# Block 1 with a plain output projection and a later store, block 3 with a tile of products moved ahead

## The reference, cut to what matters

```python
def retention_layer(h, w_in, w_out):
    q, k, v, g = jnp.split(h @ w_in, [1024, 2048, 4096], axis=-1)   # 4 heads: q, k 256 wide, v, g 512
    ...                                    # rope, chunkwise recurrence over 64-token chunks, giving o
    o = (o - mean(o)) * rsqrt(var(o) + EPS)                          # per head
    return (o * silu(g)) @ w_out                                     # 2048 -> 1024

h = h + retention_layer(rmsnorm(h, ret_norm), ret_w_in, ret_w_out)
kb, vb = shared_kv(h, kv_norm, w_kv)
h = h + swa_sink_layer(rmsnorm(h, swa_norm), swa_w_in, sinks, swa_w_out, kb, vb)
out = rmsnorm(h, final_norm)
```

## Time and profile before

| | us |
|---|---|
| median of 3 runs (2570.06 to 2570.86) | 2570.57 |
| profiled execution, time | 2570.57 |
| profiled execution, span | 2568.7 |
| PE busy | 2412.4 (94%) |
| PEld busy | 1978.0 (77%) |
| DVE busy | 1476.4 (57%) |
| ACT busy | 680.2 (26%) |
| POOL busy | 429.9 (17%) |

### The profile page before, as it was taken

How to read it: one execution, slowest core, us unless ns; L and a number is a source line. 1 busy time by engine, 2 the same in 40 slices (tenths; PEclk the granted TensorE clock), 3 DMA queues, 4 the chain that set the end, 5 groups by cost and what they waited for, 6 DMA issues and landing times.

```text
span 2568.7 us, 28654 instructions
## 1 busy us (share of the span) xinstructions
PE 2412.4 (94%) x11216; PEld 1978.0 (77%) x11216; DVE 1476.4 (57%) x2034; ACT 680.2 (26%) x1470; POOL 429.9 (17%) x326
## 2 busy tenths in 40 slices
PE   7999999999886869697999999999999999999998
PEld 6888888877675657486888888888888887887886
DVE  6555556586454536365376746557385756556374
ACT  2221312244120202022253312213153312222243
POOL 2112112220452524352001100001001000000000
PEclk9999999999998989898999999999999999999999
DMA  8657575637786858586427887786436987787433
GB/s 350 266 199 307 216 278 212 246 115 302 284 316 245 337 215 335 228 323 239 170 101 256 314 281 263 260 267 239 164 126 224 325 277 257 250 276 253 173 109 147
DMA packets 131833, 625.84 MB, mean 244 GB/s; under 512 B 8864, under 2 KB 9632, under 8 KB 109728
## 3 DMA queue, kind: packets, MB, share of 16 engines
q1 hardware_dynamic: 122864, 588.53, 63.2%
q10 hardware_dynamic: 8880, 36.18, 3.8%
HBM read 471.58 MB, written 153.09 MB: 243 GB/s over the span
## 4 chain that ended last, share of the span: by engine, by line
PE 81%; DVE 7%; DMA 6%; POOL 2%; issue 2%; SPq 1%; ACT 1%; DVEq 0%; ACTq 0%; POOLq 0%
PE ps L686 26%; PE ps L688 25%; PE ps L687 25%; DMA whl<-split_w 2%; DMA whl<-comb_w 2%; PE ps L1195 2%; DVE ff L1955 1%; DMA comb_w<-ff 1%; POOL raw L631 1%; DVE ff L2248 1%; POOL ff L640 1%; PE ps L1205 1%; SPq L468 1%; DVE fr L1658 1%; DVE fr L1654 1%
## 5 line engine op out<-in xcount | busy, mean ns | idle before, releaser
L686 PE MATMUL ps<-whl,xhi 128*128 128x512 f32 (+1 forms) x1088 | 419.0, 385 | 20.5 <-DMA whl<-split_w 18.6
L688 PE MATMUL ps<-whl,xlo 128*128 128x512 f32 (+1 forms) x1088 | 413.3, 380 | 0.0
L687 PE MATMUL ps<-whl,xhi 128*128 128x512 f32 (+1 forms) x1088 | 412.0, 379 | 0.0
L686 PE MATMUL ps<-xhi,whl 128*128 128x512 f32 x768 | 308.4, 402 | 81.4 <-DMA whl<-split_w 63.7
L688 PE MATMUL ps<-xhi,whl 128*128 128x512 f32 x768 | 303.8, 396 | 0.0
L687 PE MATMUL ps<-xlo,whl 128*128 128x512 f32 x768 | 303.4, 395 | 0.0
L686 PE MATMUL ps<-whl,fr 128*128 128x512 f32 x640 | 258.8, 404 | 21.7 <-DMA whl<-comb_w 19.4
L688 PE MATMUL ps<-whl,fr 128*128 128x512 f32 x640 | 255.6, 399 | 0.0
L687 PE MATMUL ps<-whl,fr 128*128 128x512 f32 x640 | 254.2, 397 | 0.0
L686 PEld LDWEIGHTS ps<-whl,xhi 128*128 128x128 f32 x1088 | 206.6, 190 | 58.6 <-DMA whl<-split_w 19.0
L688 PEld LDWEIGHTS ps<-whl,xlo 128*128 128x128 f32 x1088 | 206.3, 190 | 39.0
(11 more groups left out here) (215 smaller groups left out, 3826.8 us busy)
## 6 DMA issues: line engine op xcount, KB each, us to landing
whl<-split_w SPq DMA_DIRECT2D x60, 2048.0 KB, 7.9
whl<-split_w SPq DMA_DIRECT2D x118, 1024.0 KB, 6.8
split_w<-whl SPq DMA_DIRECT2D x44, 2048.0 KB, 7.3
whl<-vg_w SPq DMA_DIRECT2D x64, 1024.0 KB, 6.8
raw<-in_stream SPq DMA_DIRECT2D x44, 1024.0 KB, 9.4
vg_w<-ff SPq DMA_DIRECT2D x32, 1024.0 KB, 7.6
whl<-comb_w SPq DMA_DIRECT2D x32, 1024.0 KB, 6.6
raw<-in_stream SPq DMA_DIRECT2D x50, 512.0 KB, 9.2
```

The source lines that it names most:

```text
L686: pe.matmul(dst, lhs[0], rhs[0], start=start, stop=False)
L687: pe.matmul(dst, lhs[0], rhs[1], start=False, stop=False)
L688: return pe.matmul(dst, lhs[1], rhs[0], start=False, stop=stop)
```

## The change

1. **Block 1, projection.** The seven products go; `one_head` now does for block 1 what it did for block 0 alone: chunks 6 and 7 whole, 96 matmuls, four splits of `y` and eight adds. Gate tiles and transposes go in order 0, 1, 2, 3 and no longer 2, 3, 0, 1. `y_sums_lo` on GpSimd runs only in later blocks.
2. **Block 1, order on SP.** Chunks 6 and 7 are loaded next to each other behind piece 5, then store 4 and piece 0 of the next head. Store 5 of a head is handed on (`last_store`) and issued in the next head behind its chunk 1, with piece 1 behind it, ahead of chunk 2; for the last head, behind the second chunk of the post part. The wait for all stores moves behind the post part's loads.
3. **Block 3.** The first of the two tiles of `vg_product(S1, 15, 1, 0)` is issued ahead of `inner(3)`, the second stays behind `cross(3)`.

```diff
@@ combining_head (SP)
                 for c in range(3):
                     load_split(at, c, split_rows(h, c), CHUNK)
+                    if c == 1 and h > 0:
+                        last_store()
+                        load_piece(h, 1)
...
-                sp.wait_ge(o_mm.sem, at(o_mm, 4))
-                load_comb(t4hl, T4)
-                load_comb(t3hl, T3)
-                for c, q, first in ((6, T1, 0), (7, T2, HALF)):
-                    sp.wait_ge(w_used.sem, at(w_used, c - 1))
-                    load_comb(whl[c % 2][:, :, 0:HALF], q)
-                    sp.dma_start(whl[c % 2][:, :, HALF:].bitcast(F32),
-                                 split_rows(h, 6)[:, :, first:first + HALF]).then_inc(w_ready[c % 2].sem, 16)
-                    if c == 6:
-                        store_piece(4)
-                        if h < HEADS - 1:
-                            load_piece(h + 1, 0)
-                sp.wait_ge(yt_mm.sem, at(yt_mm, 4))
-                sp.dma_start(b22hl.bitcast(F32), split_rows(h, 7)[:, :, HALF:]).then_inc(b22_loaded.sem, 16)
-                store_piece(5)
+                for c in (6, 7):
+                    load_split(at, c, split_rows(h, c), CHUNK)
+                store_piece(4)
                 if h < HEADS - 1:
-                    load_piece(h + 1, 1)
+                    load_piece(h + 1, 0)
+                return lambda: store_piece(5)
@@ post_loads (SP)
+                    if c == 1 and last_store is not None:
+                        last_store()
@@ GpSimd, block 1
-                    y_sums_lo(at)
-                    if b < FAST:
                         comb_piece(at, 5)
+                    else:
+                        y_sums_lo(at)
@@ one_head (PE): winograd() is gone, and for blocks 0 and 1
+                    w_wait(at, 5)
+                    for t in range(TT):
+                        over_tokens(t, t, 5, DV, xs, 4, 4, False, True).then_inc(g_mm.sem if t < 3 else w_used.sem, 1)
+                        if t >= 1:
+                            transpose_y(t - 1)
+                    for n in range(2):
+                        w_wait(at, 7 + n - 1)
+                        w = chunk_view(6 + n, 4)
                         for t in range(TT):
+                            pe.wait_ge(yt_lo.sem, at(yt_lo, t + 1))
+                            for e in range(4):
+                                mm = three(ps[:, 4 * n + t, :], [v[:, e, t * P:(t + 1) * P] for v in ythl],
+                                           [v[:, e, :] for v in w], e == 0, e == 3)
+                            mm.then_inc(out_mm.sem if t < 3 else w_used.sem, 1)
+                            if n == 0 and t == 0:
+                                transpose_y(3)
@@ fast_head (PE), last block only
                     else:
+                        vg_product(S1, 15, 1, 0, (0,), ends=False)
                         pe.wait_ge(v_lo.sem, at(v_lo, 4))
                     inner(3, True)
                     cross(3, False)
-                    vg_product(S1, 15, 1, 0)
+                    vg_product(S1, 15, 1, 0, (1,) if last else (0, 1))
@@ post part (PE)
-                pe.wait_ge(h_add.sem, at(h_add, -8 if first else -2))
+                pe.wait_ge(h_add.sem, at(h_add, -8 if b < FAST else -2))
```

More of the change, by code:

```diff
@@ L319, in build @@
         x_part_lo = count("x_sums_lo", post=4, since=FAST)
[L320 to L325, removed]
+        p1_copied = count("product_copied", head=1, since=FAST)
+        a21_copied = count("y_part_copied", head=1, since=FAST)
+        a_sum = count("y_sums", head=4, since=FAST)
+        a_hi = count("y_parts_hi", head=7, since=FAST)
+        a_lo = count("y_parts_lo", head=3, since=FAST)
+        s_parts_lo = count("y_sums_lo", head=4, since=FAST)
         kv_mm = count("kv_tile", post=3)
@@ L550, in post_loads @@
                                  split_w[n * P:(n + 1) * P, :, 0:width(n)]).then_inc(ready[c % 2].sem, 16)
-            for b in range(1, BLOCKS):
-                for h in range(HEADS):
-                    if b < FAST:
[L555 to L560, removed]
+                    if c == 1 and last_store is not None:
+                        last_store()
+            last_store = None
+            for h in range(HEADS):
+                last_store = combining_head(1, h, last_store)
+            post_loads(1, last_store)
+            sp.wait_ge(comb_stored.sem, Place("head", 1, HEADS - 1)(comb_stored, 2 * PIECES))
+            for b in range(FAST, BLOCKS):
+                for h in range(HEADS):
+                    fast_head(b, h)
                 post_loads(b)
@@ L831, in transpose_y @@
                     def transpose_y(t):
-                        pe.wait_ge(y_done.sem, at(y_done, 1 + (t if first else LATE_FIRST.index(t))))
+                        pe.wait_ge(y_done.sem, at(y_done, t + 1))
                         for e in range(4):
@@ L835, in transpose_y @@
                         tr.then_inc(yt_mm.sem, 1)
[L838 to L890, removed]
@@ L892, in one_head @@
-                    if first:
-                        w_wait(at, 5)
-                        for t in range(TT):
[L895 to L913, removed]
+                    w_wait(at, 5)
@@ L941, in x_lhs, with vg_product @@
                         return [v[:, (0 if a == A11 else 4) + k, tok] for v in xs]
-                    def vg_product(a, pos, half, bank, tiles=(0, 1), tile_done=None):
+                    def vg_product(a, pos, half, bank, tiles=(0, 1), tile_done=None, ends=True):
                         if tiles[0] == 0:
@@ L953, in vg_product @@
                                 mm.then_inc(tile_done.sem, 1)
-                        if tile_done is None:
+                        if tile_done is None and ends:
                             mm.then_inc(half_used.sem, 1)
@@ L1493, in one_head @@
                                        bias=obias[:, t:t + 1]).then_inc(o_norm.sem, 1)
-                    def gate_silu(n):
-                        t = LATE_FIRST[n]
-                        if n < 3:
-                            act.wait_ge(g_mm.sem, at(g_mm, n + 1))
+                    for t in range(TT):
+                        if t < 3:
+                            act.wait_ge(g_mm.sem, at(g_mm, t + 1))
                         else:
@@ L2061, in gate_y @@
                         dve.wait_ge(o_norm.sem, at(o_norm, t + 1))
-                        dve.wait_ge(g_silu.sem, at(g_silu, 1 + (t if first else LATE_FIRST.index(t))))
+                        dve.wait_ge(g_silu.sem, at(g_silu, t + 1))
                         dve.tensor_tensor(on[:, t, :], on[:, t, :], sg[:, t, :], ALU.mult).then_inc(y_done.sem, 1)
@@ new lines, in one_head @@
+                    gate_y(0)
+                    gate_y(1)
+                    split_yt(0)
+                    gate_y(2)
+                    split_yt(1)
+                    gate_y(3)
+                    split_yt(2)
+                    add_to_h(0, 0)
+                    split_yt(3)
+                    if first:
+                        split_chunk(n0 + 7)
+                    add_to_h(0, 1)
+                    add_to_h(0, 2)
+                    add_to_h(0, 3)
+                    if first:
+                        split_chunk(n0 + 8)
@@ L2176, in one_head @@
+                    for t in range(TT):
+                        add_to_h(1, t)
+                    if combine:
                         comb_less_hi(5)
```

123 lines of the change are left out of this document (6 added, 117 removed).

## The result

The changed kernel takes 2470.8 us (median of 4 runs, 2469.33 to 2472.86) against 2570.65 us before: ratio 0.9613, 95% interval 0.9596 to 0.9629. 99.8 us are gone. The forecast was 2469.4 us, the range 2460 to 2482. The profiled execution after has a span of 2469.8 us.

What follows compares the result with a forecast made beforehand. TensorE was taken to wait in block 1 for loads queued behind `store_piece(5)` on SP. Gains of 97.4 us in block 1 and 3.7 in block 3, together 101.1 off 2570.57, gave 2469.4 us, range 2460 to 2482.

Steps and rivals of the forecast that it cites:

- The clock T: Block 1: a head's start had it begun at full rate, dated 32.7 us before K's transposes; T = 934.0.
- root to next start: Block 1, from a head's inverse root to the next head's first products with the plain projection: 37.2 us.
- Chunks 6, 0 and 2: Block 1 loads: chunks 6 and 0 land in time, chunk 2 at T+22.0 against T+21.8, a 0.2 us stall.
- The price of 2.76 us per MiB: SP's load queue in block 1: each further MiB costs 2.76 us, on a fixed part of 2.4 us.
- Start to root: Block 1, from a head's start to its inverse root: 72.1 us as before, plus 1.3 in heads 1 to 3.
- the charge: Block 1, heads 1 to 3: 1.3 us each, of which GpSimd slowing VectorE's `comb_less_hi(0)` is 1.1 us.
- The seam: End of block 1: from its last product to the key transposes 29.3 us, so these come at 1128.4 against 1225.84.
- Part 1: Block 1, plain projection and moved store 5: gains 97.4 us, 82 in three periods, 15 behind the last root.
- Part 2: Block 3, one tile ahead of `inner(3)`: gains 0.9 us a head, 3.7 in four; bounds 0 and 5.4.
- carry long trains slower: Rival, block 1's queue: 344 GB/s, 3.05 us per MiB, 9.1 us more, 2478.5 us; chance 20%.
- chain back: Rival, block 1 heads 1 to 3: VectorE waits for pieces ahead of V's low part, 6.4 us each, 2488.6; chance 8%.
- The slower rival: Block 1's transfers become the bound: 34 MiB a head at 228 GB/s take 156 us, total 2607; chance 2%.

## Why the prediction was right

*The bound.* That SP's order made the long waits is shown: the early store costs 76 us with the plain projection, the late one takes 78 away with the seven products. Store 5 and piece 1 moved together in both.

*The clock T, and root to next start.* Forecast 37.2 us; measured 37.6 to 37.7 (842.35 to 912.68 - 32.7). The assumption that the gate, its transposes and the splits keep their durations held to 0.5 us; where the 0.5 went was not looked for.

*Chunks 6, 0 and 2* were to be there in time or 0.2 us late, and no wait for them is in the trace. Chunk 2 lands 21.4 to 21.6 us behind the head's start; forecast 22.0, wanted at 21.8. The price of 2.76 us per MiB held for five MiB (16.1 us in the run with the early store), for seven (21.5 us from the issue of chunk 1 to chunk 2's landing, 21.7 by the forecast's sum) and for one more (2.1 to 3.0 us).

*Start to root.* Forecast 73.4 us, with 1.3 charged on the 72.1 of before; measured 72.5, 72.2 and 73.7, the last in a head where the clock fell (see the end). In the two heads at full clock the charge was worth 0.4 and 0.1 us. The collision came as forecast (3.38 us against 3.4), store 0 left 20.9 us behind the start (forecast 19.4 and the 1.1), and chunk 3 came 0.8 to 1.0 us late. What the forecast left out is that the kernel before lost nearly as much in the same stretch to V's low part, a wait that the changed kernel does not have (TensorE's timeline of the kernel before, head 2):

```profile
982.08 0.47 PE L686 MATMUL ps<-fr 128*128 128x512 f32 x1 [0.71 <-DVE fr L1658]
```

So the mechanism was right as far as chunk 3, and the term was too large by about 1 us a head.

*The seam.* Root to key transposes in the last head: forecast 37.2 + 29.3 = 66.5 us, measured 66.9.

*Part 1 in all:* forecast 97.4 us, measured 97.4 from the first root on. That they agree to 0.1 us is luck: root to next start came out 1.5 us longer in three heads, start to root 1.8 us shorter (1.5 us of fallen clock included), the seam 0.4 us longer. Part 2: forecast 3.7, measured 3.6. The remainder to the measured 99.8 us lies ahead of the first root, in the low clock of one execution, and in the scatter of the runs.

*The rivals.* The queue did not carry long trains slower: between 780 and 790 us it moved 417 GB/s, and 419 between 800 and 810. That speaks again against some 358 GB/s for the HBM side of a core's transfers (the Trainium skill, DMA: Bandwidth & Descriptors, Where 436 GB/s comes from) as a bound of this kernel, which runs alone. The pieces did not chain back in the changed kernel, but they did as soon as piece 1 came later, by 0.7 to 2.4 us a head and not the 6.4 of the rival's price. The slower rival had no part.

*Where I was off more* is in an experiment: I gave the place of the store 87 us and the plain projection 10, and they were worth 78 and 17.5. One error in it is a last product read off the chain (1045.94) and not off TensorE's own timeline (1048.7), 2.8 us a head. Of the 8.8 us by which that run missed its forecast, 2.7 lie ahead of its first root (732.80 against 730.05) and have nothing to do with it.

## What to carry to other kernels

On a queue that issues in order, ask of each store what load stands behind it and when the store can leave, and how many bytes then go ahead of it, not how many flow in all: here the same 34 MiB a head cost one wait of 19.1 us or one of 0.8 by the place of 3 MiB. A form with fewer products has to pay for its extra operands at the point where they are due: here 12 matmuls saved 2.7 us and the wait for their weights cost 5.8, and some 2 us at the low clock. When a wait is filled with work from behind it, look for the chain that starts at its end: one tile gained 0.9 us a head, two lost 0.3.

## What the runs showed of the hardware that I had not expected

A stretch at a lower clock can stand behind a small wait, in one head and not in its twin. Two heads of the same code, each with a wait of 0.8 us for chunk 3 and two that sum to 1.0 or 1.1 us for gated y, differ by 1.5 us from start to root, and the granted clock does too. In the changed kernel it was full throughout head 2, and in head 3 it fell for a stretch (by-stretch view; the column before the last two is the clock, 1.00 being 2.4 GHz and 0.50 1.2 GHz):

```profile
1020.00:1030.00 10.00, 9.21 (x53) 7.94 (x52) 5.73 (x4) 1.66 (x2) 7.66 (x5) 0.88 1.03 418
1030.00:1040.00 10.00, 10.00 (x44) 8.25 (x43) 4.36 (x4) 2.07 (x3) 6.27 (x4) 0.95 1.03 408
```

The fall begins within a microsecond of the end of the 0.8 us wait (granted clock 0.75 from 1027 to 1028 us, 0.50 behind it). In the run without block 3's edit the same fall came in head 2 instead (0.89 and 0.94 from 910 to 930 us, roots 111.6 us apart against 110.7 and 110.5). In the run with one MiB more, a wait of 2.1 us in head 1 was followed by full clock (1.00 from 790 to 810 us). Behind the 4 us wait of head 0 the clock fell in every execution looked at, but the first product took 0.50 us in three of twelve and 0.80 in the others. What picks the head was not found, nor is it shown that the wait is the cause. It puts 1 to 1.5 us of scatter on a head, as much as the last experiments were after.

Where VectorE and GpSimd met, the one that began later lost. In the earlier trace rows GpSimd began at 964.82 and VectorE at 964.89, which took 3.37 us for its usual 2.28. In the changed kernel GpSimd's subtractions began at 786.63 and VectorE's low part at 787.32: it took 3.38 us. In the run with one MiB more VectorE began 0.36 us ahead of GpSimd and lost nothing, while GpSimd's first subtraction took 3.07 us, where the shortest of the four took 1.27 (timelines of VectorE and GpSimd):

```profile
787.43 2.28 DVE L1862 TENSOR_TENSOR ff<-raw,ff 128x2048 fp32r<-128x2048 f32 x1
...
787.79 7.46 POOL L622 TENSOR_TENSOR raw<-raw 128x512 f32<-128x512 f32 x4 [3.17 <-DMA raw<-in_stream]
```
